# Triangle products of stick-breaking attention in two fp32r passes over halves of the softplus

## The reference

```python
z = einsum("bqhd,bkhd->bhqk", q, k) * scale
mask = s_idx < t_idx
log_not = where(mask, -softplus(z), 0.0)
after = cumsum(log_not, axis=3, reverse=True) - log_not
w = where(mask, exp(log_sigmoid(z) + after), 0.0)
out = einsum("bhqk,bkhd->bqhd", w, v)
```

## Time and profile before

| | |
|---|---|
| median of 3 runs | 3319.55 us (3316.45 to 3319.96) |
| profiled execution | 3313.52 us, span 3312.4 us |
| PE busy | 3199.0 us |
| VectorE busy | 2052.8 us |
| ScalarE busy | 1359.3 us |
| GpSimd busy | 1349.4 us |
| the stage, first layer | about 473.0 to 531.6 us |
| the stage, second layer | about 1524.5 to 1583.1 us |

### The profile page before, as it was taken

The page is one execution under the profiler, slowest core; times in us unless marked ns, Lnnn a source line. Parts: engine busy times, 40 slices in busy tenths (PEclk is TensorE's granted clock), DMA queues, the critical chain, the costliest instruction groups (busy, mean ns, idle before and its releaser), DMA issues.

```text
span 3312.4 us, 50521 instructions
## 1 busy us (share of the span) xinstructions
PE 3199.0 (97%) x19480; PEld 2724.8 (82%) x19487; DVE 2052.8 (62%) x2671; ACT 1359.3 (41%) x2335; POOL 1349.4 (41%) x643
## 2 busy tenths in 40 slices
PE   8999999999999999999999999998999999999998
PEld 6998875789977899877579987765689987879987
DVE  6774444577646876355477765678477733477753
ACT  5553225344435455322434543324434531154542
POOL 6320562544116541065174404656554107735300
PEclk9999999999999999999999999999999999999999
DMA  4543221145332454322025533211145433215532
GB/s 156 157 148 106 89 88 33 64 152 158 116 124 83 129 169 122 105 83 89 14 102 153 157 115 113 102 64 39 45 140 155 135 106 110 83 46 153 163 117 96
DMA packets 99965, 362.50 MB, mean 109 GB/s; under 512 B 11088, under 2 KB 11344, under 8 KB 99536
## 3 DMA queue, kind: packets, MB, share of 16 engines
q1 hardware_dynamic: 88704, 320.90, 29.0%
q0 software_dynamic: 7776, 28.32, 5.1%
q10 hardware_dynamic: 3312, 10.86, 0.9%
HBM read 355.84 MB, written 4.19 MB: 109 GB/s over the span
## 4 chain that ended last, share of the span: by engine, by line
PE 76%; DVE 9%; POOL 4%; ACT 4%; issue 4%; DMA 3%; DVEq 0%; ACTq 0%; POOLq 0%; SPq 0%
PE psC L754 4%; PE psC L756 4%; PE psC L755 4%; PE psA L754 4%; PE psA L756 4%; PE psA L755 4%; PE psD L904 2%; PE psD L906 2%; PE psD L905 2%; PE psB L904 2%; PE psB L906 2%; PE psB L905 2%; PE psC L904 2%; PE psC L906 2%; PE psC L905 2%
## 5 line engine op out<-in xcount | busy, mean ns | idle before, releaser
L634 POOL TENSOR_TENSOR WH<-raw,scalars 128x1024 fp32r<-128x1024 f32 (+1 forms) x194 | 379.1, 1954 | 1192.3 <-DMA raw<-in_w 1127.0
L2247 DVE TENSOR_TENSOR WL<-raw,WH 128x1024 fp32r<-128x1024 f32 x324 | 441.4, 1365 | 74.6 <-POOL raw L668 46.4
L636 POOL TENSOR_TENSOR WL<-raw,WH 128x1024 fp32r<-128x1024 f32 (+1 forms) x194 | 472.4, 2435 | 15.2
L1702 ACT ACTIVATE WH<-raw 128x1024 fp32r<-128x1024 f32 x324 | 340.7, 1054 | 37.4 <-DMA raw<-in_ws 25.8
L2323 DVE TENSOR_TENSOR WL<-raw,WH 128x1024 fp32r<-128x1024 f32 (+1 forms) x144 | 163.1, 1135 | 291.9 <-ACT WH L1723 291.5
L663 POOL TENSOR_TENSOR raw<-raw,Y 128x1024 f32<-128x1024 f32 x54 | 133.7, 2476 | 509.1 <-DMA raw<-in_ws 509.1
L1723 ACT ACTIVATE WH<-raw 128x1024 fp32r<-128x1024 f32 (+1 forms) x144 | 141.8, 988 | 346.4 <-DMA raw<-in_w 346.4
L754 PE MATMUL psA<-HH,WH 128*128 128x512 f32 x560 | 229.9, 410 | 0.0
L756 PE MATMUL psA<-HL,WH 128*128 128x512 f32 x560 | 218.4, 390 | 0.0
L755 PE MATMUL psA<-HH,WL 128*128 128x512 f32 x560 | 218.0, 389 | 0.0
L904 PE MATMUL psD<-TH,WH 128*128 128x256 f32 x720 | 200.6, 279 | 2.3 <-ACT psD L1742 2.0
(11 more groups left out here) (536 smaller groups left out, 9622.1 us busy)
## 6 DMA issues: line engine op xcount, KB each, us to landing
raw<-in_w SPq DMA_DIRECT2D x338, 512.0 KB, 3.5
raw<-in_ws SPq DMA_DIRECT2D x216, 512.0 KB, 3.6
Y<-in_ws SPq DMA_DIRECT2D x54, 512.0 KB, 4.6
raw<-in_ws POOLq DMA_DIRECT2D x54, 512.0 KB, 5.4
X<-in_x ACTq DMA_DIRECT2D x4, 512.0 KB, 9.9
NRAW<-in_mem ACTq DMA_DIRECT2D x2, 1024.0 KB, 6.8
out<-Y SPq DMA_DIRECT2D x8, 256.0 KB, 2.1
POSI<-in_pos ACTq DMA_DIRECT2D x4, 256.0 KB, 2.6
```

The lines of the kernel that those rows point to most:

```text
L634: pool.tensor_tensor(WH[j][:, 0:w], raw[j][:, 0:w], zero[:, 0:1].broadcast_to([P, w]), ALU.subtract).then_inc(w_hi, 1)
L636: pool.tensor_tensor(WL[j][:, 0:w], raw[j][:, 0:w], WH[j][:, 0:w], ALU.subtract).then_inc(w_split, 1)
L1702: act.activation(WH[slots[i]][:], DX if i == 6 else raw[slots[i]][:], ACT.Copy).then_inc(part_hi, 1)
L2247: dve.tensor_tensor(WL[slots[i]][:], DX if i == 6 else raw[slots[i]][:], WH[slots[i]][:], ALU.subtract).then_inc(part_lo, 1)
```

## The change

`r` now makes two passes for each unit, with fp32r operands: first the triangle and ones matrices (a fp32r copy, SBC) times SBH, the high part of the softplus, then times SBLOW, the rest. ScalarE makes SBH with one copy for each unit, placed after the weights of the pair before. VectorE makes SBLOW in the place of SBL by a subtraction for each unit, `low`, placed after the pair's two `softplus`; it also copies the matrices to SBC once in each layer. PE waits for `sb_hi` ahead of a unit's first pass and for `sb_lo` ahead of its second.

```diff
+    SBH = sb("SBH", [P, 2, 10 * P], F32R, offset=HLo)
+    SBC = sb("SBC", [P, 2, P], F32R, offset=HLo + 10 * KB)
+    SBLOW = sb("SBLOW", [P, 2, 10 * P], F32R, offset=Yo)
...
-                pe.wait_ge(zsp_ready, n.full(zsp_ready))
-                for k in range(b, QB):
-                    o = sb_bank(i)[:, (k - b) * P:]
-                    at = slice(sb_at(k), sb_at(k) + sb_w(k))
-                    mm = pe.matmul(o, tri if k == b else onen, SBL[:, x, at], start=False, stop=k == QB - 1, skip_group_check=True)
+                if i == 0:
+                    pe.wait_ge(sb_const, n.full(sb_const))
+                pe.wait_ge(sb_hi, n.full(sb_hi))
+                for part in (SBH, SBLOW):
+                    if part is SBLOW:
+                        pe.wait_ge(sb_lo, n.full(sb_lo))
+                    for k in range(b, QB):
+                        o = sb_bank(i)[:, (k - b) * P:]
+                        at = slice(sb_at(k), sb_at(k) + sb_w(k))
+                        mm = pe.matmul(o, SBC[:, 0 if k == b else 1], part[:, x, at], start=False, stop=part is SBLOW and k == QB - 1,
+                                       skip_group_check=True)
                 mm.then_inc(e_ready, 1)
...
                 for i in older:
                     weight(i)
+                for i in units:
+                    act.wait_ge(zsp_ready, n.full(zsp_ready))
+                    act.activation(SBH[:, i % 2, sb_part(i)], SBL[:, i % 2, sb_part(i)], ACT.Copy).then_inc(sb_hi, 1)
...
+            def low(i):
+                dve.wait_ge(sb_hi, n.full(sb_hi))
+                part = sb_part(i)
+                dve.tensor_tensor(SBLOW[:, i % 2, part], SBL[:, i % 2, part], SBH[:, i % 2, part], ALU.subtract).then_inc(sb_lo, 1)
+
+            dve.tensor_copy(SBC[:].rearrange("p a n -> p (a n)"), cf[:, C_TRI:C_ONEN + P]).then_inc(sb_const, 1)
...
                 softplus(2 * u + 1)
+                low(2 * u)
+                low(2 * u + 1)
```

More of the change, by code:

```diff
@@ L259, in program @@
     bf_ready, tf_ready, th_ready, tl_ready = map(sem, ("bf_ready", "tf_ready", "th_ready", "tl_ready"))
-    w_hi = sem("w_hi")
+    w_hi, sb_hi, sb_lo, sb_const = map(sem, ("w_hi", "sb_hi", "sb_lo", "sb_const"))
     w_split = sem("w_split")
```

## The result

The changed kernel takes 3327.57 us, median of 20 runs (3318.69 to 3342.38), against 3317.65 us of the kernel before (20 runs): a ratio of 1.003, with a 95% interval of 1.002 to 1.0039. It is slower by 0.3%, where 2.3 us more and no measurable change were forecast. The profiled executions differ by 12.1 us of span, 3324.5 against 3312.4.

What follows compares the result with a forecast made beforehand. PE was taken to set the pace, with its chain waiting on VectorE and ScalarE at two places. Per layer 0.3 us lost plus 0.9 for the clock, 2.3 us in all, gave 3321.9 us, range 3312 to 3328.

Steps and rivals of the forecast that it cites:

- pairs 1 and 3: Triangle products of these pairs: savings of 0.44 us and 1.75 us land in each layer.
- pairs 4 and 5, with the hold: Savings of 0.20 and 0.44 us land, less 1.0 us for pair 5's subtractions meeting GpSimd's splits.
- Prices: fp32r passes on PE: 0.23, 0.17, 0.12 and 0.11 us for 512, 384, 256 and 128 columns.
- The third rival: 128-column passes cost 0.06 us, total 3320.1, or 0.23 us, total 3326.3; chance 0.13 together.
- Half: 1.0 lost: Pair 5: nothing lost if VectorE gets between GpSimd's two splits, about 2 us if not; half was taken.
- 0.9 a layer: Pair 7's last three passes at a low clock after PE's idle time: between nothing and 1.85 us, 0.9 taken.
- some 2 us earlier: Sign of being right: z of pair 7 comes this much sooner after the first z; 1.8 us in the sum.
- 2.1 us more than 7.26: Pair 7, end of z to end of products: this much longer, behind ScalarE's copies and subtractions held by GpSimd.
- A latent piece waiting for its eviction: Sign of being wrong: PE's next latent piece held up by VectorE's eviction, a wait the forecast didn't have.
- Without the hold (the first): Rival: subtractions not held up and the clock holds; 2.4 us gained a layer, 3314.7 us; chance 0.20.
- The slower side: Rival: clock stays low behind pair 7 through the first scores and `pv` in one layer; 3327.7 us; chance 0.17.
- all 14.2 us arrives: Rival: the whole PE saving of both layers shows in the time, 3305.3 us; chance 0.05.

Runs made afterwards that it cites:

- e1: Changed kernel, but GpSimd's splits that meet the subtractions wait until these are done; 3311.88 us against 3311.68 of the kernel before, ratio 1.0001.
- e2: Changed kernel plus unused fp32 products on PE during its waits in pairs 5 and 7, subtractions still held; 3316.75 us, ratio 1.0006 to the kernel before.
- e8: The changed kernel run again unaltered, on another chip; 3324.99 us, ratio 1.0028 to the kernel before.
- e6: Changed kernel's copies, subtractions and waits, but with the fp32 products of the kernel before and the halves unused; one run of 3337.77 us.
- e5: Changed kernel without the low-half product and its subtraction, ScalarE's copy kept; span 3313.7 us, stages 53.9 and 53.8 us.
- e9: Changed kernel with units 8, 10, 12 and 14 kept on the fp32 product, no GpSimd waits; 3313.05 us, ratio 1.0003 to the kernel before.
- e3: Changed kernel with both GpSimd waiting for the subtractions and unused fp32 products in pairs 5 and 7; 3311.68 us, ratio 0.9991 to the kernel before.

## Why the prediction was right and where it was wrong

The mechanism was right: serial work ahead of pair 7 and a hold in pair 5 take back what the faster passes save. The size was wrong: the point was 2.3 us over the kernel before, and the stages show 10.9. That the range held the time, by 0.4 us, is luck: the forecast started from 3319.55 us, and the kernel before came out at 3317.65 over all its runs; 9.9 us on top of 3319.55 lie outside. By the prediction's own bound of 6.6 us the change counts as slower, to which it gave 0.19, and not as no change, to which it gave 0.67. By the terms of the sum, first layer, in us (a minus is a gain):

| term | predicted | measured |
|---|---|---|
| pairs 1 and 3 | -2.19 | -1.65 |
| pairs 4 and 5, with the hold | +0.36 | +1.48 |
| behind pair 5 to the end of pair 7's z | 0 | +1.76 |
| pair 7, with the hold and the clock | +3.0 | +3.70 |
| sum | +1.2 | +5.29 |

**Prices.** Right. Pair 1's eight records take 0.93 us for 0.92 forecast, and passes of 128 columns start 0.11 apart. The third rival is out on both sides. Pair 3 lands 0.54 short together with pair 1, and most of that is the wait between its first two passes: its subtraction was held to 1.11 us, as allowed for, and the passes start at 502.87 and 504.00, 0.50 more than the 0.63 of one, instead of the 0.1 that was counted.

**The hold in pair 5.** "Half: 1.0 lost" is the first term that was mis-sized. VectorE got in between L637 and L639 with one subtraction, the other waited for all of L639: 1.48 plus the 0.20 and 0.44 that pairs 4 and 5 save makes 2.1 us, the whole price and not half of it. Both layers of both profiles of the changed kernel show the wait (1.49 to 1.67 us), and e1 takes it away. The two subtractions were due one behind the other; "gets in between" could serve one of them, so the mean of the two cases was no case.

**The clock.** The second term. Its 0.9 a layer stood for pair 7 alone. There the low clock costs 1.37 us, 3.43 against the 2.06 of e2. What the sum has no row for is the 1.54 us of standing in pair 5, behind which seven products ran at half speed. That is most of the 1.76 in the table, though e8 shows that it does not come each time. So z of pair 7, which the sum has 1.8 us earlier and the signs "some 2 us earlier", ended 1.59 us later. The Trainium skill (TensorE: Matmul & The Clock Gate, Part 1) has the clock low unless sustained work releases it. In pair 7 the traces agree: after a wait of 3.42 us the granted clock was 0.54 in the changed kernel and 0.77 in e1. Behind pair 5 the first profile agrees (0.57 after 1.54 us), but e8 and e6 show 1.00 after waits of 1.49 and 1.60 us.

**Pair 7.** "2.1 us more than 7.26": 3.70 less the 1.37 of the clock is 2.3. The wait of 3.4 us and the second one behind the held subtraction came as forecast.

**The wait that was named as a sign of being wrong.** "A latent piece waiting for its eviction" did come, behind the held subtractions of pair 2:

```profile
500.46 0.50 PE L757 MATMUL psC<-CH,WH 128*128 128x512 f32 x1 [1.01 <-DVE PROJ L2425]
```

It cost nothing, as the chain runs through ScalarE at that time (L1903 to L1924, up to 502.83). Behind pair 5 such a wait is on the chain: the 0.15 us of the transposes for the eviction L2429.

**The rivals.** Without the hold (the first), e1 gives 57.6 and 58.3 us, so 0.9 and 0.3 gained a layer for its 2.4, mainly because the clock falls in pair 7 without the hold too: its four passes take 3.72 and 4.35 us, for the 2.52 of the forecast. The slower side came true in its sign: more PE work ran at the lower clock than the sum has, but not behind pair 7 through the scores as that rival had it. It ran behind pair 5 and in pair 7. That all 14.2 us arrives is out: e5, with half the passes and no subtraction, gains 4.6 and 4.7 us a layer.

Left open: why the clock fell behind pair 5 in one execution and held in another after nearly the same wait.

## What to carry to other kernels

A faster product that needs a prepared operand can be slower on the path: count from the last producer to the first product, not the products alone. Use the new form where other work covers the preparation, and keep the old one for the unit that has to start at once. When a two-input VectorE instruction meets long GpSimd instructions, cost it at the end of the GpSimd instruction, for each of them, and let GpSimd's work wait where the buffers allow it.

## What was new about the hardware

A VectorE instruction with two SBUF operands that starts under a GpSimd split ends only after it. In e9 a subtraction of 512 columns was due at 529.38, GpSimd ended at 531.05, and VectorE ended at 531.59, 0.54 us later; the earlier trace rows show the same 0.54. With 256 columns it is 0.28 us: pair 5's second subtraction ended at 518.42, L639 at 518.14. The Trainium skill (SBUF — State Buffer, SBUF: two separate sides) calls the shared port pair an exclusive lock that whoever starts first holds for the whole instruction. The rows agree: 4.01 us for two subtractions that take 0.76 when GpSimd stands aside.

Idle fp32 products on PE kept the granted clock at 1.00 in pair 7 (e2), where the changed kernel, after PE had stood for 3.42 us, shows 0.54, close to the lower of its two levels. They delay the next pass where the gap is shorter than they are (e3).
